# Attention scores for four heads at once, with plain and rotary features laid apart

## What is computed

```python
def _mla_qkv(c_q, c_kv, k_rope, q_a_g, w_uq, kv_a_g, w_ukv, q_norm_g, k_norm_g, rope):
    b, n, _ = c_q.shape
    q = (_rmsnorm(c_q, q_a_g) @ w_uq).reshape(b, n, A_HEADS, A_QK)
    kv = (_rmsnorm(c_kv, kv_a_g) @ w_ukv).reshape(b, n, A_HEADS, A_NOPE + A_V)
    k_nope, v = kv[..., :A_NOPE], kv[..., A_NOPE:]
    k_r = jnp.broadcast_to(k_rope[:, :, None, :], (b, n, A_HEADS, A_ROPE))
    k = jnp.concatenate([k_nope, k_r], axis=-1)
    q = _rmsnorm(q, q_norm_g)
    k = _rmsnorm(k, k_norm_g)
    if rope is not None:
        q = jnp.concatenate([q[..., :A_NOPE], _apply_rope(q[..., A_NOPE:], rope)], axis=-1)
        k = jnp.concatenate([k[..., :A_NOPE], _apply_rope(k[..., A_NOPE:], rope)], axis=-1)
    return q, k, v

def _attend(q, k, v):
    s = jnp.einsum('bqhd,bkhd->bhqk', q, k).astype(jnp.float32) * (A_QK ** -0.5)
    p = jax.nn.softmax(s, axis=-1).astype(v.dtype)
    return jnp.einsum('bhqk,bkhd->bqhd', p, v)
```

## Time and profile before

| | us |
|---|---|
| median of 3 runs | 878.61 |
| lowest, highest | 878.52, 880.6 |
| profiled execution | 880.03 |
| its span | 878.2 |
| PE busy | 858.1 (98%) |
| DVE busy | 637.8 (73%) |
| ACT busy | 448.5 (51%) |

### The profile page before, as it was taken

How to read it: one execution, slowest core, us unless ns; L and a number is a source line. 1 busy time by engine, 2 the same in 40 slices (tenths; PEclk the granted TensorE clock), 3 DMA queues, 4 the chain that set the end, 5 groups by cost and what they waited for, 6 DMA issues and landing times.

```text
span 878.2 us, 13397 instructions
## 1 busy us (share of the span) xinstructions
PE 858.1 (98%) x5364; PEld 710.6 (81%) x5364; DVE 637.8 (73%) x1256; ACT 448.5 (51%) x763; POOL 23.5 (3%) x19
## 2 busy tenths in 40 slices
PE   8999999999999999999999999999999999999996
PEld 4678578776686888778998888989999888888885
DVE  4534879675656789966699999978588765565665
ACT  3353545554633564655443544556554765555552
POOL 0000000000000000000003113000000000000000
PEclk9999999999999999999999999999999999999999
DMA  9785543202173135213665665532366365645541
GB/s 351 306 308 190 216 186 114 85 1 77 44 263 110 35 103 170 84 45 112 197 203 167 193 194 179 155 120 72 108 205 207 118 207 190 207 167 202 186 174 48
DMA packets 40717, 138.25 MB, mean 157 GB/s; under 512 B 4432, under 2 KB 4560, under 8 KB 40400
## 3 DMA queue, kind: packets, MB, share of 16 engines
q1 hardware_dynamic: 40224, 134.41, 45.3%
q10 hardware_dynamic: 432, 3.00, 0.9%
HBM read 136.34 MB, written 1.05 MB: 156 GB/s over the span
## 4 chain that ended last, share of the span: by engine, by line
PE 65%; DVE 26%; ACT 4%; DMA 2%; issue 2%; SPq 0%; DVEq 0%; POOLq 0%; POOL 0%; ACTq 0%
DVE wlo L1507 9%; PE ps L412 9%; PE ps L987 6%; DVE AF L2025 6%; PE ps L413 4%; PE ps L367 3%; PE ps L749 3%; PE ps L368 3%; PE ps L372 3%; PE ps L384 2%; DMA AF<-wmod 2%; PE ps L487 2%; PE ps L772 2%; PE ps L395 2%; PE ps L385 2%; PE ps L386 2%
## 5 line engine op out<-in xcount | busy, mean ns | idle before, releaser
L1027 ACT ACTIVATE whi<-raw 128x1024 fp32r<-128x1024 f32 (+3 forms) x213 | 211.5, 1002 | 99.3 <-DMA raw<-wpack 58.4
L1507 DVE TENSOR_TENSOR wlo<-raw,whi 128x1024 fp32r<-128x1024 f32 (+3 forms) x213 | 240.9, 1154 | 27.4 <-ACT whi L1027 27.2
L367 PE MATMUL ps<-hx,whi 128*128 128x256 f32 (+1 forms) x384 | 115.4, 301 | 0.5 <-ACT AF L1383 0.3
L412 PE MATMUL ps<-hx,whi 128*128 128x512 f32 x320 | 113.9, 398 | 0.0
L368 PE MATMUL ps<-hx,whi 128*128 128x256 f32 (+1 forms) x384 | 112.0, 292 | 0.0
L372 PE MATMUL ps<-hx,wlo 128*128 128x256 f32 (+1 forms) x332 | 96.9, 292 | 0.0
L413 PE MATMUL ps<-hx,wlo 128*128 128x256 f32 x320 | 89.8, 281 | 0.0
L367 PEld LDWEIGHTS ps<-hx,whi 128*128 128x128 f32 x384 | 73.4, 191 | 4.2 <-issue 2.3
L368 PEld LDWEIGHTS ps<-hx,whi 128*128 128x128 f32 x384 | 73.4, 191 | 2.0 <-issue 0.7
L457 PE MATMUL ps<-whi,hx 128*128 128x512 f32 (+1 forms) x192 | 71.8, 374 | 0.9 <-DVE lat L1643 0.9
L412 PEld LDWEIGHTS ps<-hx,whi 128*128 128x128 f32 x320 | 60.1, 188 | 14.6
(11 more groups left out here) (319 smaller groups left out, 1677.9 us busy)
## 6 DMA issues: line engine op xcount, KB each, us to landing
raw<-wpack SPq DMA_DIRECT2D x181, 512.0 KB, 4.1
AF<-wmod SPq DMA_DIRECT2D x48, 512.0 KB, 6.6
raw<-wpack SPq DMA_DIRECT2D x24, 256.0 KB, 3.1
raw<-wpack SPq DMA_DIRECT2D x6, 384.0 KB, 3.0
XT<-xin SPq DMA_DIRECT2D x4, 512.0 KB, 6.7
raw<-wpack SPq DMA_DIRECT2D x4, 432.0 KB, 5.5
cst<-cpack ACTq DMA_DIRECT2D x1, 1349.0 KB, 8.6
AF<-l2rows ACTq DMA_DIRECT2D x1, 1024.0 KB, 7.5
```

The lines of the kernel that those rows point to most:

```text
L367: e.matmul(o, wh[:, b], xh(k), start=j == 0, stop=False, skip_group_check=True)
L412: e.matmul(ps.ap(key, 512).rearrange("p (s n) -> p s n", s=2), wh[:, b], K.hx[:, :, k, 0:256], start=k == 0, stop=False, skip_group_check= ...
L1027: e.activation(W.hi(i), W.raw(i), ACT.Copy).then_inc(*HI.up(j))
L1507: e.tensor_tensor(W.lo(i), W.raw(i), W.hi(i), ALU.subtract).then_inc(*LO.up(j))
```

## The change

Queries and keys are laid out with all heads' plain features first (512 columns of a tile) and all rotary ones behind (256), by reordering the columns of the weights. `heads_T` makes six full 128x128 transposes, four of plain features (two heads each, one bank, evicted by ACT) and two of rotary features (four heads each, one bank, evicted by DVE as 256 columns). Scores are made for four heads at once, when i % 4 is 0: four matmuls of 32 rows, one on each quarter of the rows, then four of 64 rows on the two halves, each pair of matmuls of a head summed in one bank. The four banks are always 0 to 3; all else takes banks 4 to 7 until the last item (`ps.low`). The rotary part of the keys is turned and multiplied by its gain once per tile (`key_turns`, seven small DVE operations) and its squares are summed once (four small ACT operations); keys are no longer turned per head. `q_proj(1)` moves from step 8 to the end of step 3, with its squares, sums, scaling and turns; the transposes of keys from steps 6 and 7 to 7, of the queries from 15 and 17 to 11 and 15. ACT does `exps(i)` ahead of `pt(i - 3)` except in each fourth step, and the projections that end in steps 3, 7, 11, ... are evicted in the same step (`soon`).

```diff
@@ -119,11 +119,11 @@
...
     def begin(self):
-        self.clock, self.holder, self.held, self.age = 0, [None] * 8, set(), [0] * 8
+        self.clock, self.holder, self.held, self.age, self.low = 0, [None] * 8, set(), [0] * 8, 0
 
     def take(self, key, n=1, hold=False, at=None):
 
-        free = [i for i in (range(9 - n) if at is None else (at,)) if not any(j in self.held for j in range(i, i + n))]
+        free = [i for i in (range(self.low, 9 - n) if at is None else (at,)) if not any(j in self.held for j in range(i, i + n))]
...
@@ -312,6 +320,11 @@
 
 BESIDE = (halves(*(("agate", m, 2 * m, 2 * m + 1) for m in range(4)), ("ggate", 0, 9, 11), ("gu", 0, 13, 15), ("ggate", 1, 17, 19), ("gu", 1, 21, 23), ("gws", 0, 24, 24)),
           halves(*(("agate", m, 2 * m, 2 * m + 1) for m in range(4)), ("gu", 1, 8, 10), ("gws", 0, 11, 11)))
+
+
+def soon(l, i):
+
+    return i % 4 == 3 and i in BESIDE[l] and BESIDE[l][i][2] and BESIDE[l][i][0] != "gws"
 
 
 def fills(i):
@@ -657,11 +670,12 @@
 
         def heads_T(nm, p, x, y):
             pe.wait_ge(V[l, "rope", nm, p, y] if p else V[l, "rope", nm, p])
-            for h0 in (0, 4):
-                key = (l, nm + "T", p, y, h0)
+            for part, c, n in (("n", 0, 4), ("r", 512, 2)):
+                key = (l, nm + "T", p, y, part)
                 pe.wait_ge(*ps.take(key))
-                for j in range(4):
-                    i = e.transpose(ps.ap(key, P, j * P, slice(0, 96)), g.X[x][:, y * 768 + (h0 + j) * 96:y * 768 + (h0 + j + 1) * 96], C("ident"))
+                for j in range(n):
+                    a = y * 768 + c + P * j
+                    i = e.transpose(ps.ap(key, P, j * P), g.X[x][:, a:a + P], C("ident"))
                 i.then_inc(*M.up(key))
 
         def spatial():
@@ -742,11 +756,18 @@
...
         def scores(i):
+
             t, h = items[i]
             n = (2 if t < 2 else 4) * P
-            key = (l, "s", i)
-            pe.wait_ge(*K.heads_done(l, "q", t // 2, t % 2), *K.heads_done(l, "k", 0), *(K.heads_done(l, "k", 1) if t >= 2 else []), *ps.take(key))
-            e.matmul(ps.ap(key, n), g.Q[0:96, t % 2, h, :], g.K[0:96, h, 0:n], start=True, stop=True, skip_group_check=True).then_inc(*M.up(key))
+            pe.wait_ge(*K.heads_done(l, "q", t // 2, t % 2), *K.heads_done(l, "k", 0), *(K.heads_done(l, "k", 1) if t >= 2 else []))
+            pe.wait_ge(*(x for j in range(4) for x in ps.take((l, "s", i + j), at=j)))
+            for j in range(4):
+                r = slice(32 * j, 32 * j + 32)
+                e.matmul(ps.ap((l, "s", i + j), n), g.Qr[r, t % 2, h // 4, :], g.Kr[r, h // 4, 0:n], start=True, stop=False, skip_group_check=True)
+            for j in range(4):
+                r = slice(64 * (j % 2), 64 * (j % 2) + 64)
+                e.matmul(ps.ap((l, "s", i + j), n), g.Qn[r, t % 2, (h + j) // 2, :], g.Kn[r, (h + j) // 2, 0:n],
+                         start=False, stop=True, skip_group_check=True).then_inc(*M.up((l, "s", i + j)))
 
         def turned(i):
             nk = 2 if items[i][0] < 2 else 4
@@ -780,20 +801,11 @@
         mt, mht = (lambda k: V[l, "mix", k]), (lambda k: A[l, "oh", tiles[-1]])
         half = None
         for i in range(ni + 4):
-            if i < ni:
+            ps.low = 4 if i < ni - 1 else 0
+            if i < ni and i % 4 == 0:
                 scores(i)
             if 0 <= i - 3 < ni:
                 turned(i - 3)
-            if l == 0 and i == 8:
-                q_proj(1)
-            if l == 0 and i == 6:
-                heads_T("k", 1, 0, 0)
-            if l == 0 and i == 7:
-                heads_T("k", 1, 0, 1)
-            if l == 0 and i == 15:
-                heads_T("q", 1, 0, 0)
-            if l == 0 and i == 17:
-                heads_T("q", 1, 0, 1)
             if i >= 5 and i % 2:
                 values(i - 5)
             if i in BESIDE[l]:
@@ -806,6 +818,13 @@
...
                         M.mark(("hread", l))
+            if l == 0 and i == 3:
+                q_proj(1)
+            if l == 0 and i == 7:
+                for y in range(2):
+                    heads_T("k", 1, 0, y)
+            if l == 0 and i in (11, 15):
+                heads_T("q", 1, 1, i // 15)
             if i in BEGUN[l]:
                 m = BEGUN[l][i]
                 begun.append(lin_first((l, "wout", m), "w_out", l, (P * m, P), 4, xh, xl, N, mt))
@@ -1278,29 +1307,31 @@
...
         ni = len(items)
         for i in range(ni + 4):
+            if i < ni and i % 4:
+                exps(i)
             if 0 <= i - 3 < ni:
                 pt(i - 3)
-            if i < ni:
+            if i < ni and i % 4 == 0:
                 exps(i)
-            if i - 1 in BESIDE[l] and (BESIDE[l][i - 1][2] or BESIDE[l][i - 1][0] == "gws"):
+            if i - 1 in BESIDE[l] and not soon(l, i - 1) and (BESIDE[l][i - 1][2] or BESIDE[l][i - 1][0] == "gws"):
                 beside(*BESIDE[l][i - 1][:2])
             if l == 0 and i == 0:
-                squares("k", 1, 0, 2, V[l, "krb", 1], V[l, "gvr"])
-            if l == 0 and i == 6:
-                heads_T("k", 1, 0, 0)
+                squares("k", 1, 0, 2, V[l, "gvr"])
+            if soon(l, i):
+                beside(*BESIDE[l][i][:2])
             if l == 0 and i == 7:
-                heads_T("k", 1, 0, 1)
-            if l == 0 and i == 8:
-                highs((l, "uq", 1, 0))
-                q_take(1, 0, M[l, "kT", 1, 1, 4])
-            if l == 0 and i == 9:
-                squares("q", 1, 0, 2, V[l, "rope", "k", 1])
-            if l == 0 and i == 15:
-                heads_T("q", 1, 0, 0, M[l, "s", 7])
-            if l == 0 and i == 17:
-                heads_T("q", 1, 0, 1, M[l, "s", 15])
+                for y in range(2):
+                    heads_T("k", 1, 0, y)
+            if l == 0 and i in (11, 15):
+                heads_T("q", 1, 1, i // 15, M[l, "s", 8 * (i // 15) + 7])
             if i in BESIDE[l] and BESIDE[l][i][0] != "gws":
                 highs((l, *BESIDE[l][i][:2]))
+            if l == 0 and i == 2:
+                highs((l, "uq", 1, 1), 0)
+            if l == 0 and i == 3:
+                q_take(1, 1, M[l, "qT", 0, 1, "r"])
+            if l == 0 and i == 4:
+                squares("q", 1, 1, 2, V[l, "ksum", 1])
             if 0 <= i - LATE[l] < 4:
                 mix_high(i - LATE[l])
             for t in tiles:
@@ -1730,12 +1761,27 @@
...
+        def key_turns():
+
+            kr, kx = (x[:, 0:128].rearrange("p (t n) -> p t n", t=4) for x in (g.kr, g.krx))
+            part = g.krt[:, 0:64].rearrange("p (t a b n) -> p t a b n", t=2, a=2, b=2)
+            x4 = kr[:, 2:4, :].rearrange("p t (a b n) -> p t a b n", a=2, b=2)
+            tb, g32 = tab[1]
+            gs = tb[:, 64:128].rearrange("p (t a b n) -> p t a b n", t=2, a=2, b=2)
+            dv.wait_ge(A[l, "gv", 3], V[l, "tab"])
+            e.tensor_tensor(kx[:, 2:4, :], kr[:, 2:4, :], tb[:, 0:64].rearrange("p (t n) -> p t n", t=2), ALU.mult).then_inc(*V.up())
+            for hf in range(2):
+                e.tensor_tensor(part[:, :, :, hf, :], x4[:, :, :, 1 - hf, :], gs[:, :, :, hf, :], ALU.mult).then_inc(*V.up())
...
@@ -1769,31 +1815,34 @@
...
+            if nm == "k":
+                e.tensor_reduce(ss, g.scr[z][:, 0:1024].rearrange("p (g d) -> p g d", d=64), AX.X, ALU.add).then_inc(*V.up((l, "ksum", p)))
+                s8 = ss.rearrange("p (y h) -> p y h", y=2)
+                dv.wait_ge(V.now(), V[l, "kre"])
+                e.scalar_tensor_tensor(out=s8, in0=s8, scalar=1.0 / 96, in1=g.stat[:, 8 + 2 * p:10 + 2 * p].unsqueeze(2).broadcast_to([P, 2, 8]), op0=ALU.mult, op1=ALU.add).then_inc(*V.up())
+            else:
+                e.tensor_reduce(ss, g.scr[z].rearrange("p (g d) -> p g d", d=96), AX.X, ALU.add).then_inc(*V.up())
+                dv.wait_ge(V.now())
...
+        def hscale(nm, p, x, s, ys=(0, 1)):
+
             ss, su, sw = ss_of(s)
-            Xg = g.X[x].rearrange("p (g d) -> p g d", d=96)
-            dv.wait_ge(V.now())
...
+            a, b = ys[0], ys[-1] + 1
+            s8 = ss.rearrange("p (y h) -> p y h", y=2)[:, a:b, :].unsqueeze(3)
+            Xn, Xr = g.Xn[x][:, a:b], g.Xr[x][:, a:b]
+            dv.wait_ge(V.now(), A[l, "hsq", nm, p])
+            e.tensor_tensor(Xn, Xn, s8.broadcast_to([P, b - a, 8, 64]), ALU.mult).then_inc(*V.up())
+            src = g.krx.rearrange("p (t n) -> p t n", t=4)[:, 2 * p + a:2 * p + b, :].unsqueeze(2).broadcast_to([P, b - a, 8, 32]) if nm == "k" else Xr
+            e.tensor_tensor(Xr, src, s8.broadcast_to([P, b - a, 8, 32]), ALU.mult).then_inc(*V.up())
...
@@ -1939,31 +1990,24 @@
...
-                for y in range(2):
-                    if i == 2 + 2 * y:
-                        hscale_of("k", 1, 0, 2, y)
-                    if i == 3 + 2 * y:
-                        rope("k", 1, 0, 2, y)
+                if i in (2, 3):
+                    hscale("k", 1, 0, 2, (i - 2,))
+                if i == 2:
+                    lows((l, "uq", 1, 1), 0)
```

(28 more changed lines are left out.)

124 lines of the change are left out of this document (69 added, 55 removed).

## The result

The changed kernel takes 893.98 us (median of four runs, 893.22 to 895.74) against 879.11 (four runs, 878.52 to 880.6): a ratio of 1.0165, 95% interval 1.0147 to 1.0182, about 14.5 us slower. Forecast were 882.5 us and a range up to 888. The direction was right, the size was not. The profiled execution is 895.74, its span 893.9, so 15.7 us more than the profiled one of before; that difference is followed here.

A forecast was written before the change was run, and what follows sets the result against it. PE was taken to set the pace, with DVE second. 8 us less PE work against 12 us of new waits, +4.9 - 0.85 in layer 0 and +1.65 - 1.75 in layer 1, gave +3.9: 882.5 us, range 871.5 to 888.

The forecast's parts named there:

- The work of PE: First block's attention: scores 4.5 us less at 512 keys, 0.5 at 256, transposes 3.0 less; 8.0 us in all.
- The waits of groups 1 to 3: Layer 0: waits for gate products and an eviction bring these groups to 18.6, 19.6 and 12.4 us.
- Group 7: Layer 0: group 8's scores wait for exp(27) behind DVE's late maxima; 9.63 us becomes 11.65, +2.0.
- the list of signs: Expected trace signs: score times, group distances, named PE waits, PE 8 us less busy, four calls' transposes ending 1.7 us earlier.
- the walk along DVE: Group 7 of layer 0: maxima, spatial gate and mix products in order, the last max ending at about 10.7 us.
- PE's clock falls in the new idle stretches: Rival: gaps in groups 2 and 7 slow the clock, some 1.7 us each, 884 to 888; chance 0.07.
- "-1.4" for group 8: Layer 0's last group, 27.04 us before: the waits it had mostly go, 1.4 us less.
- Groups 4 to 6: Layer 0: +0.15, -1.4 and -0.6 us, from cheaper scores, fewer or moved transposes and a bank wait in group 4.
- Ahead of layer 0's first score: Eight transposes fewer on the path before layer 0's attention: 0.85 us less.
- Layer 1's preamble: Ahead of layer 1's first score: twelve transposes fewer, 1.3 us, and shorter DVE evictions, some 0.45: 1.75 us less.
- The rival in which the 32-row matmuls don't run abreast: Each 32-row score matmul takes its own slot, +25.8 us on PE, time about 900; chance 0.03.
- The one in which waits are covered: Lighter DVE and ACT hide half or more of the 12 us: 876.6 with half, 870.6 with none; chance 0.42.

The follow-up runs named there:

- the last kernel: The changed kernel with DVE's four maxima at once, scores in any of eight banks, and values made behind the same step's half projection: 871.03 us, ratio 0.9901.
- both repairs: The changed kernel with DVE taking a group's four maxima at once and scores taking the banks taken longest ago: 880.19 us, ratio 1.000.
- the fill experiment: The changed kernel with PE's three longest idle stretches filled by useless repeated transposes of one turned item: 891.14 us, ratio 1.0135.

## Why the prediction was right or wrong

- **The work of PE (8.0 us less)** was right. Four scores take 2.99 us at 512 keys (forecast 2.9) and 1.71 at 256 (130.18 to 131.89, forecast 1.6), and the last kernel's groups 2, 3, 5, 6 and 7 are 16.41, 10.25, 11.07, 12.60 and 9.68 us where the work alone was put at 16.4, 10.2, 11.2, 12.6 and 9.1. Its span is 8.0 us below the one of before; that it is just 8.0 is luck, since from the first score on it is 8.9 us shorter and that score comes 0.9 later. The four 32-row matmuls of 512 columns take 1.07 us to the next line's start, 0.2 above one slot. The Trainium skill's figure (TensorE: Matmul & The Clock Gate, "Measured speedup vs the span model", 3.07 times) gave an estimate of 1.12 for them; with the change of row grouping counted in, this trace agrees with it to 0.05 us (3.2 times).
- **The waits of groups 1 to 3** were right: 18.50, 19.55 and 12.17 us against 18.6, 19.6 and 12.4, with the waits where they were put: turned for the gate product 1.7, head transposes 0.8, values 1.3.
- **Group 7** was right in mechanism and 1.3 us short (12.96 against 11.65). The wait fell on values (2.76 us at 229.88) and not, as the list of signs had it, on group 8's scores (0.41). The step that was mis-sized is the walk along DVE: it puts the last maximum's end at 10.7 us after the group's start; it was at 12.1 (229.84 and 0.68), since DVE also waited 0.87 us for exp 24 and the first score was there at 2.2 us.
- **The clock** is the step that failed. "PE's clock falls in the new idle stretches" stood among the rivals with 0.07, because stretches with small gaps in the rows of before showed 1.00. Those gaps were 0.3 to 0.7 us in one piece; the new ones reach 2.8. It fell behind three of them, of 2.76, 1.96 and 1.77 us. The sum priced this at nothing. The rival's own price, 1.7 us a gap, was near: one fall costs 1.5 (group 4 in the experiments with both repairs, 14.31 us with it and 12.79 without). In all it cost 3.0 us between group 8's start and layer 1, and 1.4 at the end (the fill experiment), and it turned "-1.4" for group 8 into +3.5 together with 2.0 us of values' wait at 244.20 that the sum had put at nothing.
- **Groups 4 to 6** were short by 0.8, 0.55 and 1.0 us. The sum took turned, values and projections as PE work in a row and saw a wait only where exp stood in the way; it missed that a score between turned and values had hidden ACT's eviction. In group 4 the wait of 1.4 us for the output product stood there too, larger than forecast. This is the second step that failed. Moving values is worth 7 to 10 us (the table above); the uncovered eviction alone is less, since 4.1 us of the 9 between the two profiles with both repairs are group 4's, with its clock.
- **Ahead of layer 0's first score** -0.85 was forecast and +1.7 seen. The transposes gave 0.85 back (the shift at the next line is +0.23 behind a shift of +1.05 from the clock at 86 us), and then PE waited for a transfer:

```profile
122.53 2.10 PE L500 MATMUL ps<-AF 128*32 128x512 f32 x12
124.81 1.05 PE L500 MATMUL ps<-AF 128*32 128x512 f32 x4 [0.18 <-DMA AF<-wmod]
...
130.18 0.71 PE L766 MATMUL ps<-AF 32*128 32x256 f32 x8 [0.50 <-DVE mod L1567]
```

  for the modulation weights (L500) and then for what DVE makes of them (L1567). The gain was hidden by a transfer that already stretched the same line before. How much of the 1.7 is the change cannot be said: over the profiles of the twelve kernels here that are the same up to there, the first score starts between 125.5 and 132.6 us, the middle of them at 128.4, and in the two kernels without the change at 128.1 and 128.4. So most of the 1.7 is probably this one profile's, and the forecast 0.85 isn't seen either.
- **Layer 1's preamble** came out at -1.56 against -1.75. It is all from the twelve transposes fewer (six calls, where the list of signs says four); the wait ahead of the first score, of which 0.45 was to go, is 0.65 us, for ACT's eviction now, where it was 0.68 for DVE's.
- The rival in which the 32-row matmuls don't run abreast is refuted. The one in which waits are covered did not happen with the change; the last kernel, with three further edits, is at 871.03 us, where it put 870.6 for no waits at all.

So direction and most places were right, and the size was wrong by terms that have the same sign: the clock (4.4 us in the profile), the uncovered eviction and the output product in groups 4 to 6 (2.4), values' wait in group 8 (2.0) and the late end of DVE's walk in group 7 (1.3). With the 2.6 us ahead of the first score, which are mostly this profile's own, and smaller ones of both signs they make the 12 us between +3.9 and +15.7.

## What to carry to other kernels

When several heads' scores are made at once, the matmul that used to stand between two dependent steps is gone: move other work there (here values behind a projection, 7 to 10 us), and let the engine that reads the scores read them all at once before its other duties (8 to 11 us). A forecast of idle PE must price the clock behind a gap of about 2 us or more, not the gap alone, and give one of 1.3 to 1.8 us a chance of it; one fall cost 1.5 us here (group 4 is 14.31 us with it and 12.79 without, behind the same wait). And a saving in PE's work should be looked for in the distance between the same points of both traces: here it was there to about 0.1 us in groups 1, 2, 3, 5 and 6 once the three costs were repaired.
